# The samples' queries ahead of the y norm in a two-layer decoder step on one core

## The reference

```
h    = rmsnorm(x) ; proj = h @ w_in
y    = ssd_scan(...) + d_skip * xh ; y = y * silu(z)
y    = rmsnorm(y in 2 groups of 512, ssm_norm) ; ya = y @ w_ssm_proj
q    = rmsnorm(c_q) @ w_qb              # 8 heads, 64 plain + 32 rotary
q_pe = rope(q[..., 64:]) ; q_lat = q[..., :64] x w_kb
yb   = softmax(q_lat.kv + q_pe.kr) over the past pages (samples) or the prompt, then w_vb, w_mla_proj
x    = x + (sigmoid(gate_a)*ya + sigmoid(gate_b)*yb) @ w_out
x    = x + PEER(rmsnorm(x))             # 16 gathered experts for each of 8 heads
```

## Time and profile before

| | us |
|---|---|
| median of 3 runs | 2364.79 |
| lowest and highest | 2362.98, 2364.99 |
| the profiled execution's own time | 2367.7 |
| its span, first to last instruction | 2366.2 |
| TensorE busy (share of the span) | 1989.0 (84%) |
| VectorE busy | 1518.1 (64%) |
| ScalarE busy | 452.3 (19%) |
| GpSimd busy | 637.1 (27%) |
| mean granted TensorE clock | 0.970 |

### The profile page before, as it was taken

The page is one execution under the profiler, slowest core; times in us unless marked ns, Lnnn a source line. Parts: engine busy times, 40 slices in busy tenths (PEclk is TensorE's granted clock), DMA queues, the critical chain, the costliest instruction groups (busy, mean ns, idle before and its releaser), DMA issues. The chain is left out here.

```text
span 2366.2 us, 26964 instructions
## 1 busy us (share of the span) xinstructions
PE 1989.0 (84%) x9206; PEld 1141.5 (48%) x9206; DVE 1518.1 (64%) x3836; ACT 452.3 (19%) x1360; POOL 637.1 (27%) x592
## 2 busy tenths in 40 slices
PE   5999888998988877777779997889998987777775
PEld 4887655754444312222258875567454442222221
DVE  2454433468777788888524544345787878887874
ACT  1233211021211111111122342111211121111111
POOL 0000000034444444444200000001444443544441
PEclk9999899999999999999979998999999999999998
DMA  5346389499999999999744473893999999999996
GB/s 165 119 139 226 120 284 305 149 365 399 419 420 419 415 374 420 420 412 418 306 152 146 130 246 122 282 315 131 393 410 419 419 411 413 380 420 420 420 415 247
DMA packets 188196, 744.54 MB, mean 315 GB/s; under 512 B 16338, under 2 KB 76170, under 8 KB 117376
## 3 DMA queue, kind: packets, MB, share of 16 engines
q0 software_dynamic: 83008, 581.14, 60.2%
q1 hardware_dynamic: 105040, 161.59, 20.6%
HBM read 731.40 MB, written 11.46 MB: 314 GB/s over the span
## 5 line engine op out<-in xcount | busy, mean ns | idle before, releaser
L1046 PE MATMUL ps<-arena 128*128 128x512 f32 (+1 forms) x2112 | 1016.0, 614 | 239.7 <-DVE arena L1612 234.5
L2117 POOL DMA_INDIRECT arena<-in_peer_uv,arena x528 | 603.1, 1142 | 879.6 <-PE ps L1046 728.5
L1603 DVE CUSTOM_DVE_ANT_0 arena<-arena,h 128x1024 f32<-128x1024 f32 x512 | 627.6, 1226 | 241.5 <-DMA arena<-in_peer_uv,arena 233.3
L1046 PEld LDWEIGHTS ps<-arena 128*128 128x128 f32 (+1 forms) x2112 | 366.9, 188 | 851.8 <-DVE arena L1612 527.1
L484 PE MATMUL ps<-ht_tok,wring 128*128 128x264 f32 (+2 forms) x1728 | 385.1, 380 | 10.5 <-DMA wring<-in_w_in 5.8
L484 PEld LDWEIGHTS ps<-ht_tok,wring 128*128 128x128 f32 x1728 | 315.7, 193 | 78.3 <-issue 19.5
L1913 ACT ACTIVATE arena<-arena 128x1 f32<-128x1 f32 x528 | 105.9, 203 | 1035.4 <-DVE arena L1603 1034.3
L1612 DVE TENSOR_SCALAR arena<-consts,arena 128x128 f32<-128x128 f32 (+1 forms) x528 | 181.0, 343 | 18.1 <-ACT arena L1913 17.6
L484 PE MATMUL ps<-arena,wring 128*128 128x264 f32 (+2 forms) x512 | 92.8, 338 | 0.8 <-DVE arena L1387 0.8
L2101 POOL DMA_DIRECT2D nrow<-in_norm_ffn x2 | 1.1, 533 | 342.7 <-PE ps L803 342.7
L484 PEld LDWEIGHTS ps<-arena,wring 128*128 128x128 f32 x512 | 77.7, 192 | 10.9 <-DVE arena L1387 1.3
(11 more groups left out here) (318 smaller groups left out, 1790.6 us busy)
## 6 DMA issues: line engine op xcount, KB each, us to landing
arena<-in_pages SPq DMA_DIRECT2D x256, 272.0 KB, 4.1
wring<-in_w_in SPq DMA_DIRECT2D x38, 1024.0 KB
wring<-in_peer_wq SPq DMA_DIRECT2D x18, 1024.0 KB
arena<-in_peer_uv,arena POOLq DMA_INDIRECT x528
h<-in_state_ssm POOLq DMA_DIRECT2D x16, 512.0 KB, 5.1
out<-h POOLq DMA_DIRECT2D x16, 512.0 KB, 4.9
wring<-in_w_ssm_proj SPq DMA_DIRECT2D x8, 1024.0 KB
arena<-in_w_out SPq DMA_DIRECT2D x8, 1024.0 KB, 14.9
```

Of the source, the lines that this page charges most:

```text
L1046: last = pe.matmul(ps[0:outs, SUM_BANK[t] + half, :], diag[:, n % DIAGS, 0:outs], ring[:, HOME[n % RING], D_MODEL + half * 512:D_MODEL + ( ...
L1603: dve.tensor_tensor_reduce(ring[:, HOME[k], 0:D_MODEL], ring[:, HOME[k], 0:D_MODEL], tokens, 1.0, 0.0, ALU.mult, ALU.add, dots[:, column(n ...
L2117: pool.indirect_dma_start(ring[:, HOME[k], :], None, table, bass.IndirectOffsetOnAxis(ap=idx[:, TOPK * u + j:TOPK * u + j + 1], axis=0)).t ...
```

## The change

1. One of the four rotary products (`rotary(0)`) is issued in front of the turns of y, ahead of the wait for `y_ready`; the other three stay behind the turns. VectorE makes its cosine part right after it has raised `y_ready`, and its sine part after the turned chunks, as before.
2. VectorE copies all eight latent queries in a row, writes `qs` and raises `qs_ready`. The reciprocal of the y norm comes after that, as two instructions (one per group). The eight scalings go into the first page half: four after its maxima, two after the copy of its turn, two after the copy of its values. `ring_free` no longer waits for `yt_ready`.
3. `qs` and `pts` are cleared by GpSimd, behind its state stores: `pts` after `hs_store`, `qs` after `qpe_ready`. VectorE waits for `qs_zeroed` and `pts_zeroed`.
4. The mean, the root and its inverse live in `ht_tok`, which is free there, and no longer in `arena`.

```diff
-share(ARENA_SSD, "yroot", S1 - 4 * TOKENS, 4 * TOKENS)
-assert S1 - 4 * TOKENS >= E1
...
-        ymean, yroot = (ssd("yroot")[:, k * 2 * TOKENS:(k + 1) * 2 * TOKENS].rearrange("p (g t) -> p g t", g=GROUPS) for k in range(2))
+        ymean, yroot, yinv = (shared[:, k * 2 * TOKENS:(k + 1) * 2 * TOKENS].rearrange("p (g t) -> p g t", g=GROUPS) for k in range(3))
...
+                    def rotary(m):
+
+                        b = aux.fill()
+                        aux.filled(product(ps[:, b, 0:TOKENS], lambda c: wqb[:, c, 512 + m * P:512 + (m + 1) * P], lambda c: cqt[:, c, :], 3))
+
+                    rotary(0)
                     pe.wait_ge(sem("y_ready"), 1)
...
-                    for m in (0, 2, 1, 3):
-                        b = aux.fill()
-                        aux.filled(product(ps[:, b, 0:TOKENS], lambda c: wqb[:, c, 512 + m * P:512 + (m + 1) * P], lambda c: cqt[:, c, :], 3))
+                    for m in (2, 1, 3):
+                        rotary(m)
...
                     dve.nop().then_inc(sem("y_ready"), 1)
+                    def rotary(c, dst, table):
+
+                        b = aux.read()
+                        aux.emptied(dve.tensor_tensor(dst[:, c, :], ps[:, b, 0:TOKENS], cst(table), ALU.mult))
+
+                    rotary(0, qpt, "cosf")
                     for c in range(DC):
                         b = aux.read()
                         aux.emptied(dve.tensor_tensor(zt[:, c, :], zt[:, c, :], ps[:, b, 0:TOKENS], ALU.mult))
...
+                    rotary(0, rot, "sinf")
+                    rotary(1, qpt, "cosf")
+                    rotary(1, rot, "sinf")
...
-                    ql_out(0)
-                    ql_out(1)
-                    dve.wait_ge(sem("y_root"), 1)
-                    then(dve.reciprocal(ymean, yroot))
-                    for c in range(DC):
-                        last = dve.scalar_tensor_tensor(out=zt[:, c, :], in0=zt[:, c, :], scalar=vt[:, V_NORM + c:V_NORM + c + 1], in1=ymean[:, c // 4, :],
-                                                        op0=ALU.mult, op1=ALU.mult)
-                    last.then_inc(sem("yt_ready"), 1)
-                    ql_out(2)
-                    ql_out(3)
-
                     dve.wait_ge(sem("wide_free"), 4 + marks["ql"])
                     dve.wait_ge(sem("aux_free"), 4 + aux.n)
-                    dve.wait_ge(sem("yt_ready"), 1)
                     dve.nop().then_inc(sem("ring_free"), 1)
-                    then(dve.memset(mla("qs"), 0.0))
+                    dve.wait_ge(sem("qs_zeroed"), 1)
...
                     dve.nop().then_inc(sem("qs_ready"), 1)
+                    dve.wait_ge(sem("y_root"), 1)
+                    for g in range(GROUPS):
+                        then(dve.reciprocal(yinv[:, g, :], yroot[:, g, :]))
+
+                    def y_normed(chunks):
+
+                        for c in chunks:
+                            last = dve.scalar_tensor_tensor(out=zt[:, c, :], in0=zt[:, c, :], scalar=vt[:, V_NORM + c:V_NORM + c + 1], in1=yinv[:, c // 4, :],
+                                                            op0=ALU.mult, op1=ALU.mult)
+                        if chunks[-1] == DC - 1:
+                            last.then_inc(sem("yt_ready"), 1)
...
-                    then(dve.memset(mla("pts"), 0.0))
+                    dve.wait_ge(sem("pts_zeroed"), 1)
...
                         half_maxima(i)
+                        if i == 0:
+                            y_normed(range(0, 4))
...
                         half_turns(i)
                         for at in PROMPT_LATER.get(i, ()):
                             prompt_values(*at)
+                        if i == 0:
+                            y_normed(range(4, 6))
                         half_values(i)
+                        if i == 0:
+                            y_normed(range(6, DC))
...
+                    pool.wait_ge(sem("hs_store"), 16)
+                    pool.memset(mla("pts"), 0.0).then_inc(sem("pts_zeroed"), 1)
+                    pool.wait_ge(sem("qpe_ready"), 1)
+                    pool.memset(mla("qs"), 0.0).then_inc(sem("qs_zeroed"), 1)
```

More of the change, by code:

```diff
@@ L1296, in _ @@
                         aux.emptied(dve.tensor_tensor(zt[:, c, :], zt[:, c, :], ps[:, b, 0:TOKENS], ALU.mult))
-                    for c in range(2):
-                        b = aux.read()
-                        aux.emptied(dve.tensor_tensor(qpt[:, c, :], ps[:, b, 0:TOKENS], cst("cosf"), ALU.mult))
-                        b = aux.read()
-                        aux.emptied(dve.tensor_tensor(rot[:, c, :], ps[:, b, 0:TOKENS], cst("sinf"), ALU.mult))
+                    rotary(0, rot, "sinf")
+                    rotary(1, qpt, "cosf")
+                    rotary(1, rot, "sinf")
                     for g in range(GROUPS):
@@ L1306, in _ @@
                     dve.tensor_tensor(qpt, qpt, rot, ALU.add).then_inc(sem("qpe_ready"), 1)
-                    def ql_out(q):
+                    for q in range(4):
                         for c in range(2):
```

## The result

| us | before | with the change |
|---|---|---|
| median of 7 runs | 2365.42 | 2349.74 |
| lowest, highest | 2362.98, 2378.26 | 2345.46, 2356.04 |
| profiled execution's own time | 2367.7 | 2345.68 |
| its span | 2366.2 | 2344.1 |
| TensorE busy | 1989.0 | 1976.3 |

The ratio is 0.9928, 95% interval 0.9913 to 0.9943: faster by 0.57% to 0.87%, or 13 to 21 us. The medians lie 15.7 us apart and the two profiled executions 22.0. The sum of the prediction was 20.7, its range 2339 to 2353, so time and sign lie within it, and the median is 5.7 us above the predicted time.

A forecast was written before the change was run, and what follows sets the result against it. The bound was taken as one serial chain between each layer's last sample state and first page halves. Page-loop start 12.6 plus y stage 8.1 gave 20.7 us off 2364.8, so 2344 us; range 2339 to 2353.

The forecast's parts named there:

- The norm leaves the queries' path: Between queries and first page scores: norm and clear moved away, first scores 7.8 us earlier, first maxima 6.6 us earlier.
- 6.3 us a layer: First page halves: page turn copied at about 282.0, not 288.34, and that gain kept through the page loop.
- 291.13 − 6.3 = 284.8: First page half, layer 1: second half's scores there at 284.8, just when the last two scalings end.
- term of 12.6 us: Page loop's earlier start summed over both layers, 6.3 us in each.
- GpSimd's clear: Clear of `qs` ahead of the queries: covered for 3.0 us, price bounded by 1.34 and 10.0 us, taken as no cost.
- The rotary product: In front of y's turns: one product of 1.38 us fits the 1.86 us wait, so sums come 1.4 us earlier.
- The clock in the y stage: Turns and rotary products: 10.5 us if full clock held throughout, lower end 2.8; middle of 8.1 taken, reorder included.
- Rival A: Y stage: the clock falls as before, so 8.1 us shrinks to 2.8 and the time is 2349.4; 27%.
- Rival B: Page loop: an earlier loop waits more for pages; if half its gain goes, 2350.4 us; 12%.
- C: Rival at the queries: GpSimd's clear is slow and delays them once over 3.0 us; at 16 us, 2375; 3%.
- D: Rival at the first maxima: VectorE's order still reaches them late, so no change, 2362 to 2365 us; 3%.
- E: Rival in the page loop: third half's loads freed earlier shorten page waits, 4.8 us more gain, 2339.3 us; 5%.

The follow-up runs named there:

- e1: Changed kernel with all four rotary products behind the turns again, norm's place and GpSimd's clears kept; 2350.62 us, ratio to before 0.9932.
- e4: Changed kernel again, unaltered, on the chip of e1 to e3; 2345.46 us, ratio to before 0.9914.
- e11: Changed kernel with two rotary products, not one, in front of the wait for y; 2342.10 us, ratio to before 0.9903.
- e3: Changed kernel with the clears of `qs` and `pts` back on VectorE; 2353.54 us, ratio to before 0.9942.
- e7: Changed kernel with the three late rotary products spread among the turns, behind chunks 1, 3 and 5; 2345.61 us, ratio to before 0.9916.
- e10: Changed kernel with all eight scalings right behind the reciprocals, ahead of the first maxima; 2350.51 us, ratio to before 0.9930.
- e6: Changed kernel with reciprocals behind the first maxima and first turn's copy, scalings behind first values and second maxima; 2345.58 us, ratio to before 0.9909.
- e8: Changed kernel with the edits of e6 and e7 together; 2345.05 us, ratio to before 0.9915.
- e9: e8 with the first product that reads the norm moved from page half 1 to 2, scalings spread to match; 2341.47 us, ratio to before 0.9900.
- e12: e11 with e9's places for the reciprocals, the scalings and `ssm(0)`; 2341.41 us, ratio to before 0.9897.
- e2: Kernel before with only one rotary product moved in front of the turns; 2354.70 us, ratio to before 0.9953.
- e5: Changed kernel with GpSimd clearing `qs` four times in a row; one run, 2351.16 us, no ratio.

## Why the prediction was right, and where it was off

**The norm leaves the queries' path: right in size.** First scores 7.8 us earlier were forecast; from the sums on they came 8.1 us earlier in both layers (first scores minus sums 17.46 before, 9.34 now). First maxima: forecast 6.6, measured 6.8 in the changed kernel, e1, e4 and e11. Two errors cancel in that split, and that is luck. The scores took 1.5 us and not 2.9, because they ran at the full clock this time; so VectorE was late not by 1.2 us but by 2.7 (273.79 to 276.50), 0.2 of it because the two reciprocals took 3.64 us and not 3.44.

**"6.3 us a layer" was kept only to the first maxima.** This is the step that failed: the one that said the second half's scores would be there at "291.13 − 6.3 = 284.8", as if the first half kept its pace. The second maxima came, after the sums, 4.8 us earlier in layer 1 and 4.6 in layer 2, and the fourth half's scores 4.1 and 4.6. A lateness of VectorE was in the working (1.2 us; with 2.7 it left TensorE idle for 2.25 us in front of the first exponential's turn). That the clock's fall would then lie on the rows behind it was not. Up to the copy of the turn the forecast held (2.48 us from the maxima, 2.53 before). From there the values, the scores and L847 took 1.94, 1.93 and 1.08 us in place of 1.07, 1.05 and 0.63: 2.2 us more, about what the gain lost between the first maxima (6.8) and the second (4.8). All first halves show the same. In 14 of them (changed, e1, e3, e4, e7, e10, e11, two layers each) TensorE waited 1.3 to 5.5 us in front of that turn, and in all 14 the clock was down by the end of the second scores; in the 8 with a wait of 0.30 us there (e6, e8, e9, e12) it was so once, in e9's layer 2. (In before, e2 and e5 it had fallen ahead of the first scores already.) So the wait and the fall go together; why it fell that one time stays open. The term of 12.6 us measured 8.7 (4.1 + 4.6) in the profile of the changed kernel and 9.5 in e4's.

**GpSimd's clear: right.** Its price was bounded by 1.34 and 10.0 us and taken as covered; it is 1.38 us with 1.75 us to spare. The estimate of 1.3 us, worked out from about one cycle per element in the Trainium skill's "GPSIMD Engine Reference", section 3.1, agrees with this row. e5 shows where the cover ends.

**The rotary product: right.** The turns start at the same 8.27 us after the query product as before (8.24), and in e11's trace a second one brings the sums 0.75 us forward though it delays the turns by 0.6 us.

**The clock in the y stage: right in kind, wrong as a single value.** Forecast, if held throughout: 10.5 us for both layers; measured where it held: 5.7 + 4.3 = 10.0 (e2). ("0.5 us" a chunk gives 4.0 us for eight, not the 4.2 that the sum goes by; the turns took 4.2.) I took 8.1 as a middle; in the profile of the changed kernel it was 2.7 + 4.3 = 6.9 without rounding, since layer 1 fell and layer 2 held. With one product ahead, 10 of 14 such stages held it (changed, e2 to e6, e10; two layers each); with none ahead, 0 of 4 (before, e1); with two ahead or the products spread, 10 of 10 (e7, e8, e9, e11, e12). So the chance should have been put on each stage of each execution, with an expected value, and not on the kernel. That the product matters at all rests on few stages (10 of 14 against 0 of 4 would come by chance about once in 44), and that two or spread ones hold it more safely than one is not shown (about once in 11).

**Rival A** happened in 4 of those 14 stages, layer 1 of the changed kernel's first profile among them: the stage then took 19.6 us, which is e1's 20.7 to 20.9 less the product's 1.2. It cost less than its price there, for layer 1 still saved 2.7 us and not 1.4, as the fall lasted 6.8 us and not 10.2. The Trainium skill ("TensorE: Matmul & The Clock Gate", Part 4) says of TensorE's transpose mode that the full clock doesn't engage for it. The prediction took that as a rule for these turns, and as such it is not borne out: 24 turns in a row ran at 1.00 for 4.2 us in ten stages, and in the earlier trace rows the clock rose with nothing but 16 of them behind it. No row tells whether these turns run in that mode. What made it fall in the other four, the traces don't tell.

**Rival B** (the page loop gives it back) is refuted as a rule. Over the 12 timed kernels, and the kernel before as nought, the head saved on the ruler and the time saved by the ratio go together: 10.3 us of head and 11.1 of time (e2), 15.6 and 17.0 (changed), 19.5 and 20.3 (e4), 21.5 and 23.0 (e11), 23.2 and 23.7 (e9), 25.5 and 24.4 (e12); correlation 0.97, slope 0.92 (time saved is one minus the ratio, times 2366). e1 and e10 lie highest above that line (11.9 and 11.3 us of head, 16.1 and 16.6 of time). The head is read from one execution and the ratio from several, and without the kernel before as nought the slope is 0.76; so the line says that what is saved by the fourth half is for the most part still saved at the end, and not how much of each microsecond. The later stretch of the loop says the same: in the changed kernel it is no longer than before. **C** and **D** did not happen. **E** asked for page waits 4.8 us shorter; they were shorter by 1.0 us (4.7 and 5.2, against 4.3 and 6.6).

**The size.** On the ruler the changed kernel saves 6.9 (y stage) + 8.7 (after it) = 15.6 us, and 10.0 + 9.5 = 19.5 in e4. The forecast was 20.7. Of the 5 us short in the first, 3.9 is the first halves (12.6 against 8.7) and 1.2 the y stage (8.1 against 6.9). That the profiled execution nevertheless saved 22.0 us is luck: 6.0 of them lie in the later stretch of the loop (103.1 and 101.1 us in place of 104.6 and 105.5), which no term of the forecast named.

**A version that beats both?** e9, e11 and e12 lie at 0.9897 to 0.9903, against 0.9928 and 0.9914 in the changed kernel's two measurements. All three beat the kernel before plainly; against the changed kernel their intervals overlap, so 0.1% to 0.3% is likely and not shown. e11 moves one product on TensorE and one step on VectorE, and is the one I would take for its small edit. What stays open: what decides in one execution whether the clock falls, and whether e12's shorter head is worth anything over e11's.

## What to carry to other kernels

Take work off the path of the first stage of a loop, but look at where it lands: here the reciprocals went from the queries' path to just before the first maxima, and their wait cost twice, once as idle time and again as a slower clock behind it. Fill a wait of TensorE in front of small matmuls with independent products: two products in a gap that one nearly filled still brought the sums 0.75 us forward. Price the clock as a chance for each stage and each execution. Read an edit by a distance inside the trace: one at the same clock repeats to 0.1 us from run to run (13.6 us to the first maxima, for one), where medians of a few runs do not tell 5 us apart. A long distance that takes in falls of the clock, as the head does, needs more than one profile.

## What the runs showed of the hardware

**The same program draws different clocks.** It gave 2339.71 to 2356.74 us over the 13 runs of its two measurements, and its time goes with the mean granted clock of the run. The seven of the first measurement:

```
us      2345.46 2345.68 2346.21 2349.74 2350.09 2353.79 2356.04
clock   0.977   0.977   0.976   0.975   0.975   0.971   0.968
```

Over the 13 the correlation is −0.85, with 1.45 us for each 0.001; over the 33 runs of the kernel before that stand beside e1 to e11, −0.64 and 1.2 us. Which of the two drives the other this doesn't show. The two measurements of the changed kernel, 15.7 us under the kernel before here and 22.0 us in e4, have intervals that overlap; their mean clocks differ by 0.0009, worth 1.2 us of the 4.3 between their medians, and the rest is not accounted for.

**GpSimd clears nearly at VectorE's speed**: 1.38 us against 1.34 for 1536 columns, 0.54 against 0.48 for 512, and with no visible cost to VectorE's copies from PSUM beside it (eight in 3.14 us with three clears beside them in e5, and in 3.14 us with none in e3).
